# Side stages of three transformer blocks, placed elsewhere in the engines' orders

## The reference

```python
# block 1: stick-breaking, key-choosing and differential attention on normed heads
z = einsum('bqhd,bkhd->bhqk', qb, kf) * scale
between = cumsum(log_1m_beta, axis=3, reverse=True) - log_1m_beta
w = where(mask, exp(log_sigmoid(z) + between), 0.0)
...
_, sel = lax.top_k(score, top_k)
...
p = attn_map(q1b, k1f) - lam * attn_map(q2b, k2f)
# block 2: a recurrence over the tokens beside masked softmax attention
sa = einsum('bhvk,bhk->bhv', state, -kk_t)
state = state * w_t + sa * (kk_t * a_t) + v_t * k_t
# block 3: mixing over positions, and the memory
mixed = einsum('gts,bnsgc->bntgc', ws, v) + b_s
s = einsum('bhtd,bhsd->bhts', qc, kc) * wts
h = num / maximum(abs(den), exp(-m_t))
h = (h - mu) * rsqrt(var + EPS) * hn_g
```

## Time and profile before

| what | us |
|---|---|
| median of the runs | 2628.07 |
| the runs | 2630.12, 2628.07, 2627.79 |
| the profiled run | 2626.06 |
| its span, first to last instruction | 2624.2 |
| TensorE busy in the span | 2519.7 |
| VectorE busy | 1540.4 |
| ScalarE busy | 1084.1 |
| GpSimd busy | 328.2 |

### The profile page before, as it was taken

One profiled execution on the slowest core, in us unless ns is written; L12 is line 12 of the kernel. 1 busy time (PEld: TensorE's weight loads), 2 busy tenths in 40 slices (PEclk: granted clock), 3 DMA queues, 4 the chain that ended last, 5 costly groups with the idle time before them and its releaser, 6 DMA issues.

```text
span 2624.2 us, 37785 instructions
## 1 busy us (share of the span) xinstructions
PE 2519.7 (96%) x15220; PEld 2077.0 (79%) x15220; DVE 1540.4 (59%) x2544; ACT 1084.1 (41%) x1949; POOL 328.2 (13%) x225
## 2 busy tenths in 40 slices
PE   8889899999999999999899999999999999999998
PEld 6778898999998877766577777878866777699886
DVE  4987754654445457476647787454744544676444
ACT  4465454543223253235642223254333333466323
POOL 0143210012222010000012222020000000500001
PEclk9999999999999999999999999999999999999999
DMA  4211122222323341520035664332221123233332
GB/s 172 85 54 49 57 65 65 81 89 89 95 90 89 97 145 49 175 74 2 1 105 188 206 195 134 96 105 88 81 73 56 49 89 96 73 105 105 99 95 72
DMA packets 76987, 244.91 MB, mean 93 GB/s; under 512 B 12708, under 2 KB 18213, under 8 KB 76558
## 3 DMA queue, kind: packets, MB, share of 16 engines
q1 hardware_dynamic: 69470, 215.72, 26.6%
q10 hardware_dynamic: 7344, 26.77, 3.1%
HBM read 238.25 MB, written 6.90 MB: 93 GB/s over the span
## 4 chain that ended last, share of the span: by engine, by line
PE 78%; DVE 12%; ACT 5%; issue 3%; POOL 2%; DMA 0%; SPq 0%; ACTq 0%; DVEq 0%; POOLq 0%
PE ps L659 51%; PE ps L2525 8%; PE ps L861 5%; DVE wl L392 2%; ACT wh L380 2%; PE ps L3252 2%; PE ps L3961 1%; PE ps L3052 1%; PE ps L2273 1%; DVE xl L1126 1%; PE ps L2301 1%; DVE arena L1527 1%; PE ps L2290 1%; DVE arena L3631 1%; PE ps L1231 1%
## 5 line engine op out<-in xcount | busy, mean ns | idle before, releaser
L659 PE MATMUL ps<-xh,wh 128*128 128x512 f32 (+1 forms) x2536 | 932.4, 383 | 23.7 <-DVE xl L1152 8.1
L659 PE MATMUL ps<-xl,wh 128*128 128x512 f32 (+1 forms) x2536 | 913.5, 376 | 0.0
L659 PE MATMUL ps<-xh,wl 128*128 128x512 f32 (+1 forms) x2536 | 909.6, 374 | 0.0
L392 DVE TENSOR_TENSOR wl<-ring,wh 128x1024 fp32r<-128x1024 f32 x362 | 461.7, 1276 | 483.8 <-ACT wh L380 483.0
L380 ACT ACTIVATE wh<-ring 128x1024 fp32r<-128x1024 f32 x360 | 380.4, 1057 | 822.3 <-PE ps L659 726.8
L659 PEld LDWEIGHTS ps<-xh,wh 128*128 128x128 f32 x2536 | 464.5, 189 | 143.9 <-issue 41.9
L659 PEld LDWEIGHTS ps<-xh,wl 128*128 128x128 f32 x2536 | 464.1, 190 | 89.1
L659 PEld LDWEIGHTS ps<-xl,wh 128*128 128x128 f32 x2536 | 463.1, 189 | 88.2 <-issue 5.5
L2525 PE MATMUL ps<-xh,wh 128*128 128x264 f32 (+1 forms) x816 | 254.2, 312 | 5.3 <-DVE xl L446 3.8
L1221 POOL TENSOR_TENSOR arena<-arena 128x512 f32<-128x512 f32 (+1 forms) x35 | 60.3, 1727 | 1557.9 <-ACT arena L1206 1557.9
L2525 PE MATMUL ps<-xl,wh 128*128 128x264 f32 (+1 forms) x816 | 233.6, 286 | 0.0
(11 more groups left out here) (424 smaller groups left out, 3203.8 us busy)
## 6 DMA issues: line engine op xcount, KB each, us to landing
ring<-in_weights SPq DMA_DIRECT2D x374, 512.0 KB, 3.6
arena<-in_w_ada ACTq DMA_DIRECT2D x48, 512.0 KB, 4.5
arena<-in_cmp_w SPq DMA_DIRECT2D x2, 2048.0 KB
strip_copies<-strip_scratch SPq DMA_DIRECT2D x8, 327.5 KB, 6.3
arena<-strip_copies SPq DMA_DIRECT2D x8, 264.0 KB, 4.0
out_features<-arena SPq DMA_DIRECT2D x8, 256.0 KB, 2.1
token_scratch<-arena SPq DMA_DIRECT2D x3, 512.0 KB, 6.4
arena<-token_scratch SPq DMA_DIRECT2D x12, 128.0 KB, 4.0
```

What stands on the lines that cost most here:

```text
L392: dve.tensor_tensor(flat(self.wl[:, s % 2]), flat(self.ring[:, s % RING]), flat(self.wh[:, s % 2]).bitcast(F32), ALU.subtract).then_inc(se ...
L659: last = pe.matmul(self.place(u, e), w[:, k, :], x[:, k, o:o + m], start=(k == 0 and i == 0), stop=(k == self.chunks - 1 and i == 2))
```

## The change

The numbers that place side stages are changed; no instruction of the computation is added, removed or altered. GpSimd's order stays. SyncE's changes in one place: one load of weights now stands before the five loads that bring `chunk_scratch` back, not behind them. On ScalarE the builder puts a table load wherever two neighbours need different function tables, so the order decides their number; it rises by two, both in the memory of block 3. The diff, cut to its core:

```diff
@@ PairCausal (block 2)
-            x.mask = [max(x.score + 0.16, steps[s - 3].turned[1] + 0.1) if s >= 3 else x.score + 0.16]
-            x.mask.append(x.mask[0] + 0.1)
-            x.exp = [x.mask[0] + 0.12, x.mask[1] + 0.14]
+            x.mask = [max(x.score + 0.16, steps[s - 3].turned[1] + 0.13) if s >= 3 else x.score + 0.16]
+            x.mask.append(x.mask[0] + 0.11)
+            x.exp = [x.mask[0] + 0.1, x.mask[1] + 0.14]
...
-            x.turned[0] = x.turned[1] - 0.001
+            x.turned[0] = x.turned[1] - 0.015
...
@@ PairAttention.plan (block 1)
-            x.score = max(x.at, last.mask[1] + 0.08) if s else x.at
+            x.score = max(x.at, last.mask[1] + 0.104) if s else x.at
...
-            x.mask.append(x.mask[0] + 0.12)
+            x.mask.append(x.mask[0] + 0.068)
...
-                x.turned.append(max([x.turn + 0.27 * x.width * e, done + 0.15] + [a + 0.1 for a in free]))
+                x.turned.append(max([x.turn + 0.307 * x.width * e, done + 0.238] + [a + 0.048 for a in free]))
...
@@ first_block
-    items += [(22.3 + 1.1 * n, P1[:, u, :], whole, ...
+    items += [(22.3 + 1.17 * n, P1[:, u, :], whole, ...
...
-            t = max(t, 22.0)
+            t = max(t, 21.74)
...
-    (21.15, DF_V, 4, ...), (27.15, SP_V, 2, ...)
+    (21.2, DF_V, 4, ...), (27.52, SP_V, 2, ...)
@@ second_block
-    inverse = RwkvInverse(core, rwkv, compress, TT, 0, inverse_small, 14.200000000000001)
+    inverse = RwkvInverse(core, rwkv, compress, TT, 0, inverse_small, 14.69)
...
-    scan = RwkvScan(core, N2 + 0.6, SCAN_STEP, 21.5, ...
+    scan = RwkvScan(core, 26.6, SCAN_STEP, 20.83, ...
...
-    widths = (0.32, 0.48, 0.64, 0.8)
+    widths = (0.32, 0.48, 0.64, 0.83)
@@ Memory (block 3)
-        return self.at + 3 * (n // 4) + 0.6 * (n % 4)
+        return self.at + 2.8 * (n // 4) + 0.6 * (n % 4)
...
-                yield t + 1
+                yield t + 1.22
...
-                yield t + 1.4
+                yield t + 1.36
@@ third_block
-    tokens = ValueTokens(core, (29.4, 33.3), mv, V, VT)
-    gates = MemoryGates(core, 25, 35.2, fi, FI, M4, EB, GC, rows, weights, conv, tokens)
+    tokens = ValueTokens(core, (29.71, 33.39), mv, V, VT)
+    gates = MemoryGates(core, 25.23, 35.19, fi, FI, M4, EB, GC, rows, weights, conv, tokens)
...
-                    (38, 40, 42.5, 45.3))
+                    (37.42, 40.3, 42.5, 45.13))
```

More of the change, by code:

```diff
@@ L3352, in first_block @@
              for n, u in enumerate(range(DF_Q, DF_K + 4))]
-    items += [(22.3 + 1.1 * n, P1[:, u, :], whole, core.p("q_norm_sp" if u < SP_K else "k_norm_sp"), arrived(u), "pair64", 1.0 / 64, unit(SB_K), unit(SB_K + 1))
+    items += [(22.3 + 1.17 * n, P1[:, u, :], whole, core.p("q_norm_sp" if u < SP_K else "k_norm_sp"), arrived(u), "pair64", 1.0 / 64, unit(SB_K), unit(SB_K + 1))
               for n, u in enumerate(range(SP_Q, SP_K + 2))]
@@ L3357, in first_block @@
     ends = {}
-    for kind, groups, scale, ahead in (("stick", 2, 1.0, 2.0), ("diff", 4, 0.78, 1.4), ("soft", 2, 1.0, 1.4)):
+    for kind, groups, scale, ahead in (("stick", 2, 1.0, 2.0), ("diff", 4, 0.78, 1.4), ("soft", 2, 0.99, 1.76)):
         if kind == "diff":
-            t = max(t, 22.0)
+            t = max(t, 21.74)
         for g in range(groups):
@@ L3516, in second_block @@
     cmp = Compressed(core, 18.0, proj, compress, keys, fixed.got, Q, KC, GT, X_cmp, bias, cmp_st)
-    scan = RwkvScan(core, N2 + 0.6, SCAN_STEP, 21.5, rwkv, compress, tokens, proj, inverse, cmp, AR, MM, TOK, TT, CE, RO, NVS * T,
+    scan = RwkvScan(core, 26.6, SCAN_STEP, 20.83, rwkv, compress, tokens, proj, inverse, cmp, AR, MM, TOK, TT, CE, RO, NVS * T,
                     core.area(N2 * T + 3944, 2, 64))
@@ L3689, in turn_at @@
     def turn_at(self, n):
-        return self.at + 4.6 + 0.3 * n if n < 4 else self.at + 8.5 + 0.3 * (n - 4)
+        return self.at + 4.84 + 0.33 * n if n < 4 else self.at + 8.44 + 0.36 * (n - 4)
     def sync(self, sp):
@@ L3795, in when @@
     def when(self, h, j):
-        return self.at + 2.7 + 0.9 * h + 0.2 * j if h < 2 else self.later + (h - 2) + 0.2 * j
+        return self.at + 2.43 + 0.87 * h + 0.32 * j if h < 2 else self.later + (h - 2)*1.02 + 0.23 * j
     def m_bank(self, h):
@@ L3876, in scalar @@
             for j in range(4):
-                yield self.when(h, j) + 0.15
+                yield self.when(h, j) + 0.12
                 act.wait_ge(self.arg.sem, self.arg.at(4 * h + j + 1))
@@ L3910, in vector @@
         for n in range(8):
-            yield self.when(n) + 0.15
+            yield self.when(n) + 0.07
             g, j = divmod(n, 4)
@@ L3964, in steps @@
         def steps():
-            yield self.when(0) - 0.35
+            yield self.when(0) - 0.41
             score(0)
@@ L3968, in steps @@
                 if n + 1 < 16:
-                    yield self.when(n + 1) - 0.35
+                    yield self.when(n + 1) - 0.41
                     score(n + 1)
-                yield max(self.when(n) + 0.25, self.when(min(n + 1, 15)) - 0.35)
+                yield max(self.when(n) + 0.17, self.when(min(n + 1, 15)) - 0.27)
                 add(n)
@@ L4015, in steps @@
                     continue
-                yield self.when(n) + 0.6
+                yield self.when(n) + 0.51
                 dve.wait_ge(self.sums.sem, self.sums.at(4 * h + 4))
@@ L4021, in steps @@
                 nh = self.N[:, h % 2]
-                yield self.when(n) + 1
+                yield self.when(n) + 0.98
                 dve.wait_ge(self.absd.sem, self.absd.at(h + 1))
@@ L4061, in steps @@
             for h in range(4):
-                yield self.when(4 * h + 3) + 0.5
+                yield self.when(4 * h + 3) + 0.66
                 act.wait_ge(self.sums.sem, self.sums.at(4 * h + 4))
```

62 lines of the change are left out of this document (31 added, 31 removed).

## The result

The changed kernel takes 2602.39 us (median of 4 runs, 2597.16 to 2605.95) against 2629.1 for the kernel before on the same chip; the ratio is 0.9894, with a 95% interval from 0.988 to 0.9908. The direction was right. The size was wrong by a factor of three.

The account below looks back on a forecast made before the run. TensorE's unchanged work and its waits were taken as the bound, with 104.5 us idle. Blocks won 5.8, 1.3 and 1.4, block 1 lost 2.2, tails won 2.0: 8.3 us, giving 2619.8 against 2628.07, range 2606 to 2630.

Parts of the forecast that it names:

- The tails: Whole kernel: some 13 waits more vanish than appear, each with 0.15 us of hidden matmul tail, 2.0 us won.
- the transposes for L3196: Block 1: one transpose waiting for the last output copy loses a queue longer than its wait, 0.7 us won.
- the three L2907 waits of the 3.9 us: Block 1: sums of squares waiting for ScalarE win 1.3 us at 206.61, and 0.7 in two more through shorter queues.
- 2.2, 5.0 and 2.3 us: Losses booked in blocks 1, 2 and 3, mainly for steps with less distance or filling before what they wait for.
- The two waits for L4012: Block 3's memory: waits of 1.60 and 1.39 us behind other VectorE work both go, 3.0 us won.
- The waits for GpSimd: Block 1: sums of squares that arrive before GpSimd's squares get more room, 1.9 us won; waits fall from 7.5 to 5.6.
- The split waits near 1140: Block 2: waits of 0.23 and 0.61 us for weight splits behind a 4.16 us product go, 0.8 us won.
- The 0.7 of the compression's wait (L2128): Block 2: a 1.65 us wait for the compression's blocks shrinks by 0.7, by inverse steps that now follow them.
- The scan's 2.6: Block 2's scan: waits for L2000, L2008 and one more shrink through matmuls in between and a shorter copy queue, 2.6 us won.
- The coupled case: Rival, chance 0.22: a wait that goes makes the next smaller; 20 us won across blocks 1 to 3, time 2608.
- Only moved: Rival, chance 0.13: what one piece gains the next on the same engine pays; 2 us won, time 2627.
- The scan as bound: Rival, chance 0.11: block 2's scan chain sets the time; 11 us lost there, 6 won in other blocks, time 2633.

Follow-up runs that it names:

- e4: Kernel before with only block 1's attention numbers (leads, transposes' and scores' distances) changed: 0.9951 of the kernel before.
- e6: Kernel before with only the distances inside block 1's attention steps (transposes and scores) changed, leads as before: 0.9998.
- e14: Kernel before with block 1's attention leads and starts and the distances of scores, masks and exponentials changed: 0.9967.
- e17: Kernel before with only the distances of scores, masks and exponentials in block 1's attention changed: 0.9987.
- e5: Kernel before with only the leads and starts of whole attention steps in block 1 changed: 0.9985.
- e7: Kernel before with only the distances of transposes, products and output copies in block 1's attention changed: 0.9995.
- e8: Kernel before with block 1's key choice, norm and values-by-token numbers changed, attention as before: 0.9978.
- e13: Kernel before with block 1's attention leads and starts and the distances of transposes, products and copies changed: 0.9974.
- e12: Kernel before with only block 2's attention pair distances and last width changed, scan and inverse as before: 0.999.
- e15: Changed kernel with block 2's inverse start (14.2) and scan lead (21.5) put back: 0.9893 of the kernel before.
- e11: Changed kernel with block 1's sums of squares and ScalarE's step on each 0.08 unit later: 2608.8 us, 0.9908 of the kernel before.
- e2: Kernel before with all of block 2's numbers alone changed (attention pairs, inverse, scan, widths): 2626.0 us, 0.9983.
- control: The changed kernel itself, unaltered, timed again on the same chip: 2602.7 us, 0.9886 of the kernel before.
- second trace of before: Profile from a repeat of the kernel before, nothing changed: ratio 1.0001, span 2629.0 us against 2624.2 in its first trace.

## Why the prediction was wrong

**What bounds the kernel: right.** TensorE's work stayed, its waits went. The tails were right too. In block 1 twelve waits fewer (17 for 29) went with 1.6 us less busy time on the same matmuls and the same 3.4 us lost to the clock, 0.14 each, where 0.15 was taken.

**Where the size went wrong.** For block 1 3.6 us net were forecast, and TensorE's idle time there fell by 11.4. By waits, forecast and then measured: L2907 2.0 and 2.6; the transposes for L3196 0.7 and 3.9 (3.4 of L3074, 0.5 of L3071); L3120 1.2 and 1.2; GpSimd 1.9 and none; the value products for L3164 nothing and 3.6; losses 2.2 and none that shows. So the 7.7 us of L3164, the largest group that the prediction names, stood in the sum at nothing, with a reason given for the first 2.7 of them alone.

**The first step that failed: the price of what is passed.** For the three L2907 waits of the 3.9 us I took 1.3 of the one at 206.61, which fell by 1.34, and the other two at 0.54 and 0.18, the durations of the ScalarE instructions that no longer stand ahead. ScalarE of before in front of the wait of 2.13 us at 137.14 (last line, TensorE):

```profile
132.78 0.38 ACT L3161 ACTIVATE arena<-ps 128x256 f32<-128x256 f32 x1 [0.31 <-PE ps L3074]
136.18 0.54 ACT L3187 ACTIVATE arena<-arena 128x400 f32<-128x400 f32 x1 [3.02 <-DVE arena L3135]
136.63 0.46 ACT L2907 ACTIVATE arena<-ps,con 128x264 f32<-128x264 f32 x1
...
137.14 0.71 PE L2896 MATMUL ps<-arena,con 128*128 128x264 f32 x2 [2.13 <-ACT arena L2907]
```

and of after:

```profile
134.58 0.48 ACT L2907 ACTIVATE arena<-ps,con 128x264 f32<-128x264 f32 x1 [1.23 <-PE ps L2896]
135.80 0.54 ACT L3187 ACTIVATE arena<-arena 128x400 f32<-128x400 f32 x1 [0.74 <-DVE arena L3135]
136.24 0.47 ACT L2907 ACTIVATE arena<-ps,con 128x264 f32<-128x264 f32 x1
```

L3187 lasts 0.54 us, but it held the queue for 3.56, since it waited for VectorE at the head of it. L2907 stood behind that wait, though its input, the sum that TensorE had begun at 133.68, was done at 134.29. Passing L3187 is worth the whole 2.13 us, where 0.54 was booked. No run moves L3187 alone, but in each of the four kernels with the scores' numbers (e4, e6, e14, e17) this wait is gone, and in the four of block 1 without them (e5, e7, e8, e13) it is 1.7 to 2.3 us. The former have 2.2 to 3.4 us less before 216 us, the latter none.

The same happens through two queues at 285.43, a wait of 1.90 us that I left out. VectorE of before runs the key choice (L2831, L2832) and L3147 ahead of the mask L3120:

```profile
281.51 0.44 DVE L2831 MAX8 arena<-arena 128x8 f32<-128x272 f32 x1
...
282.98 1.34 DVE L3147 SCALAR_TENSOR_TENSOR arena<-arena 128x144 f32<-128x144 f32 x1
284.24 0.43 DVE L3120 CUSTOM_DVE_ANT_0 arena<-ps,arena 128x272 f32<-128x272 f32 x1
```

ScalarE waits with L3190 for it, and the copy L3164 that TensorE wants stands behind (last line, TensorE):

```profile
284.71 0.52 ACT L3190 ACTIVATE arena<-arena 128x272 f32<-128x272 f32 x1 [2.47 <-DVE arena L3120]
285.14 0.19 ACT L3190 ACTIVATION_READ_ACCUMULATOR arena<-arena 128x1 f32 x1
285.23 0.15 ACT L3164 ACTIVATE arena<-ps 32x4 f32<-32x4 f32 x1
...
285.43 0.27 PE L3084 MATMUL ps<-arena 128*128 128x4 f32 x1 [1.90 <-ACT arena L3164]
```

In e8, which has the later key choice and no attention number of after, TensorE's wait is down to 0.30:

```profile
281.05 0.39 PE L3084 MATMUL ps<-arena 128*128 128x4 f32 x2 [0.30 <-ACT arena L3164]
```

I had followed that edit to one L3120, the 1.2 us at 272.14, and not to the ScalarE step behind the next.

The 3.4 us of L3074, of which I counted 0.7, are the same again. At 407.65 the copy L3196 stood behind the norm's pieces, the first of which waited for TensorE (last line, TensorE):

```profile
405.53 0.48 ACT L2907 ACTIVATE arena<-ps,con 128x258 f32<-128x258 f32 x1 [1.97 <-PE ps L2896]
406.04 0.64 ACT L2913 ACTIVATE arena<-arena 128x516 f32<-128x516 f32 x1
406.71 0.63 ACT L2914 ACTIVATE arena<-arena 128x516 f32<-128x516 f32 x1
407.25 0.26 ACT L3196 ACTIVATE arena<-ps 128x128 f32<-128x128 f32 x1
...
407.65 0.41 PE L3074 MATMUL ps<-con,arena 128*128 128x128 f32 x2 [1.04 <-ACT arena L3196]
```

The products that the copy takes (L3087) were done at 403.64. In after the copy runs ahead of them:

```profile
392.99 0.26 ACT L3196 ACTIVATE arena<-ps 128x128 f32<-128x128 f32 x1
393.62 0.48 ACT L2907 ACTIVATE arena<-ps,con 128x258 f32<-128x258 f32 x1 [0.36 <-PE ps L2896]
394.12 0.64 ACT L2913 ACTIVATE arena<-arena 128x516 f32<-128x516 f32 x1
```

**The second step that failed: losses were counted apart.** I booked 2.2, 5.0 and 2.3 us because something stood closer to what it waits for, each with everything else as it was. In block 1 the booked loss shows alone in the trace of e7 (1.8) and not in its runs, and turns into a gain of 2.8 by the traces, 1.8 by the runs, once leads and scores move too. In block 2 e12 has the attention moves that were to cost most of the 5.0 and is about 3.5 faster in the scan. In block 3 the transposes (L3906) lose nothing, and the squares (L4078), given a queue longer by 0.9, stand ahead of their neighbours in after in the one head that waited, the third, where before they stood behind. ScalarE of before:

```profile
2082.90 1.06 ACT L380 ACTIVATE wh<-ring 128x1024 fp32r<-128x1024 f32 x1 [4.50 <-PE ps L659]
2083.87 0.58 ACT L3658 ACTIVATE arena<-ps 128x512 f32<-128x512 f32 x1
2084.34 1.14 ACT L4078 ACTIVATE arena<-arena 128x512 f32<-128x512 f32 x2
```

and of after:

```profile
2061.89 1.15 ACT L4078 ACTIVATE arena<-arena 128x512 f32<-128x512 f32 x2 [2.97 <-DVE arena L4034]
2062.95 1.05 ACT L380 ACTIVATE wh<-ring 128x1024 fp32r<-128x1024 f32 x1
2063.90 0.57 ACT L3658 ACTIVATE arena<-ps 128x512 f32<-128x512 f32 x1
```

That was a misreading of the order.

**Terms one by one.** The two waits for L4012, 3.0 us: gone, right, and there is no wait for L392 in their place, so the price of nothing for the norm passes held. The table loads cost nothing that shows.

The waits for GpSimd, 7.5 to 5.6 forecast: wrong, 7.5 again. The term itself was right: the three waits that it was worked out for went from 1.64, 1.58 and 0.32 us to 0.30, 1.39 and none, 1.85 won for 1.9, and in e8, without the attention's numbers, all waits for GpSimd sum to 4.2. But the one at 159.83 grew from 2.04 to 2.51, and new ones of 0.50 and 0.83 stand at 145.05 and 191.47 of after. These three come with the attention's numbers alone (e4 has them too, at 2.50, 0.50 and 0.85), where TensorE reaches the same sums earlier (157.32 us for 159.83 in after). With 0.97 at the first late norm the sum is what it was. So this is again a term that was counted apart.

The split waits near 1140, 0.8 forecast: wrong. One split now stands before the product of 4.16 us, the next behind the second product and its sum, and the wait is 1.03 us at 1141.10 for 0.84 in two. With the old inverse (e15) it is 0.8 again. The 0.7 of the compression's wait (L2128) was not made by the inverse: with block 2's numbers alone it stays at 1.57 of 1.65 us, and with block 1's alone, where block 2 is the same program, it falls to 1.0; in after it is 0.5. Why is open.

The scan's 2.6: L2008's 1.2 us are gone, L2000's waits are not. L2290's 2.0 us for 0.5 is the one new wait of size in the scan. The sign that was to decide for the scan as bound was misread: L2000 waited over 0.5 us in four of the 16 chunks before, not six, and does so in three after.

**The rivals.** The coupled case came nearest. It gave 2608 and 0.22. Its 11 us in block 1 are near the 13.0, its 6.6 in block 2 too many, its 2 in block 3 too few. That is partly luck. Its reason, that ScalarE's queue is mostly pieces of the same steps, fits one of the three places above (L3164 behind L3190); in the other two a norm's copy stands behind attention, and an attention copy behind a norm. That a wait that goes makes the next one smaller was not tested by itself. The reason I held against it, that the first and largest waits don't change, was true and small: 2.74 us at 119.40 became 3.03. "Only moved" is right for one edit, the later sums of e11. The scan as bound is refuted by e2 and e12.

**What stays open.** The medians differ by 27 to 30 us, the corrected spans by 22.8 and (control against the second trace of before) 23.0. The rest is low-clock time, as the runs' own granted clocks show: 29.9 us on average before, 24.1 after. The traces, 25.4 and 30.5 against 26.9 and 25.2, are too few to show it. The prediction had the clock as a matter of 1.8 us. Why the changed kernel has less of it is open; that it comes of the fewer waits is a guess that no run tests.

## What to carry to other kernels

When an instruction is moved past another on an in-order queue, price the passed one by how long it holds the head of the queue, its own wait included, and not by its duration; then look at who stands behind it on the next engine. A loss from a shorter distance is to be expected, if at all, only while the other end stays where it is, so sets of placement numbers that belong to the same steps should be tried together: here one set won nothing alone and about 2 us with the other two. Numbers of stages that share no stretch of time add, and can be tried apart.

## What the runs showed of the hardware

Low-clock time differs from run to run of one kernel: 21.0 to 42.2 us over 125 runs of the kernel before, 25.4 and 30.5 in its two traces, 20.1 to 35.8 in the traces of its variants. Without it the unchanged stretches agree within 1.3 us in block 1 and 2.1 in block 3. So an effect below 5 us is not read from one trace's span here, but from TensorE's idle time stretch by stretch, or from many runs with each one's low-clock time taken out of its span.
